# A second half's residual and norm work laid over seven feed-forward tiles instead of four, and a second buffer for its input tokens

## What is computed

```python
def rmsnorm(x, g):
    y = xf * lax.rsqrt(jnp.mean(xf * xf, axis=-1, keepdims=True) + RMS_EPS)
    return (y * g.astype(jnp.float32)).astype(x.dtype)
...
def swiglu(h, w_gu, w_down):
    g, u = jnp.split(h @ w_gu, 2, axis=-1)
    return (jax.nn.silu(g) * u) @ w_down
...
        x = x + gt_m * rmsnorm(y, g_mix_post[l])
        h = rmsnorm(x, g_ffn_pre[l]) * (1.0 + sc_f) + sh_f
        x = x + gt_f * rmsnorm(swiglu(h, ffn_w_gu[l], ffn_w_down[l]), g_ffn_post[l])
```

## Time and profile before

| | us |
|---|---|
| median of 3 runs | 1573.87 |
| lowest and highest of them | 1563.5, 1577.33 |
| the profiled execution | 1572.86 |
| its span | 1571.1 |
| PE busy in the span | 1437.6 |
| DVE busy in the span | 766.0 |
| POOL busy in the span | 637.7 |
| mean granted TensorE clock | 0.957 |

### The profile page before, as it was taken

One profiled execution on the slowest core, in us unless ns is written; L12 is line 12 of the kernel. 1 busy time (PEld: TensorE's weight loads), 2 busy tenths in 40 slices (PEclk: granted clock), 3 DMA queues, 4 the chain that ended last, 5 costly groups with the idle time before them and its releaser, 6 DMA issues.

```text
span 1571.1 us, 20512 instructions
## 1 busy us (share of the span) xinstructions
PE 1437.6 (92%) x7695; PEld 1168.9 (74%) x7695; DVE 766.0 (49%) x1045; ACT 534.0 (34%) x837; POOL 637.7 (41%) x301
## 2 busy tenths in 40 slices
PE   4777999989998999989888999999999999999994
PEld 1356776879987777767666888878877888887883
DVE  5567435894673878635878121123247211121235
ACT  4534274222212666643331232222222222232221
POOL 2524122162153644074533444445554444444450
PEclk9898999999999899989989999999999999999996
DMA  7653200312312344343312333323333433333331
GB/s 278 197 187 126 56 28 27 123 52 64 99 40 63 109 121 125 96 147 94 121 57 78 94 94 105 93 80 96 98 100 93 135 94 94 94 94 93 96 91 54
DMA packets 236698, 156.55 MB, mean 100 GB/s; under 512 B 11043, under 2 KB 222385, under 8 KB 236507
## 3 DMA queue, kind: packets, MB, share of 16 engines
q1 hardware_dynamic: 233189, 143.46, 30.4%
q10 hardware_dynamic: 3446, 12.24, 2.3%
HBM read 147.25 MB, written 8.81 MB: 99 GB/s over the span
## 4 chain that ended last, share of the span: by engine, by line
PE 75%; DVE 15%; ACT 4%; POOL 3%; issue 2%; DMA 1%; ACTq 1%; DVEq 0%; POOLq 0%
PE ps L1731 30%; PE ps L1736 15%; PE ps L1857 10%; PE ps L1860 5%; PE ps L2013 2%; PE ps L1979 2%; PE ps L1990 1%; POOL w_lo L1024 1%; PE ps L1779 1%; PE ps L1873 1%; DVE x L1630 1%; DVE a_f L1595 1%; DVE pr L1577 1%; DVE nrm L1597 1%; DVE a_f L1629 1%
## 5 line engine op out<-in xcount | busy, mean ns | idle before, releaser
L1008 POOL TENSOR_TENSOR w_lo<-raw,w_hi 128x1024 fp32r<-128x1024 f32 x152 | 371.8, 2447 | 447.3 <-ACT w_hi L639 447.2
L1731 PE MATMUL ps<-hb_hi,w_hi 128*128 128x512 f32 x832 | 331.6, 399 | 24.4 <-DVE g_t L1654 10.8
L1731 PE MATMUL ps<-hb_lo,w_hi 128*128 128x512 f32 x832 | 329.2, 396 | 0.0
L639 ACT ACTIVATE w_hi<-raw 128x1024 fp32r<-128x1024 f32 x152 | 160.0, 1053 | 186.6 <-PE ps L1736 180.1
L1736 PE MATMUL ps<-hb_hi,w_lo 128*128 128x512 f32 x832 | 210.2, 395 | 1.9 <-POOL w_lo L1008 1.9
L1731 PEld LDWEIGHTS ps<-hb_hi,w_hi 128*128 128x128 f32 x832 | 159.6, 192 | 63.5 <-DVE g_t L1654 12.4
L1024 POOL TENSOR_TENSOR w_lo<-raw,w_hi 128x1024 fp32r<-128x1024 f32 x22 | 95.1, 4324 | 228.1 <-ACT w_hi L779 228.1
L1736 PEld LDWEIGHTS ps<-hb_hi,w_lo 128*128 128x128 f32 x832 | 157.9, 190 | 37.1 <-POOL w_lo L1008 2.3
L1731 PEld LDWEIGHTS ps<-hb_lo,w_hi 128*128 128x128 f32 x832 | 159.7, 192 | 33.0
L1857 PE MATMUL ps<-ha_hi,w_hi 128*128 128x512 f32 (+2 forms) x432 | 164.6, 381 | 3.4 <-ACT w_hi L779 3.4
L1857 PE MATMUL ps<-ha_lo,w_hi 128*128 128x512 f32 (+2 forms) x432 | 161.8, 375 | 0.0
(11 more groups left out here) (245 smaller groups left out, 2115.8 us busy)
## 6 DMA issues: line engine op xcount, KB each, us to landing
raw<-in_ffn_w_gu SPq DMA_DIRECT2D x88, 512.0 KB, 3.8
ada1x<-in_ada_w SPq DMA_DIRECT2D x32, 512.0 KB, 4.0
raw<-in_ffn_w_down SPq DMA_DIRECT2D x32, 512.0 KB, 4.0
raw<-in_w_in SPq DMA_DIRECT2D x22, 512.0 KB, 3.9
ada<-in_ada_w SPq DMA_DIRECT2D x4, 2048.0 KB, 17.9
raw<-in_w_out SPq DMA_DIRECT2D x16, 512.0 KB, 4.1
raw<-in_ffn_w_down SPq DMA_DIRECT2D x16, 384.0 KB, 3.3
raw<-in_ktab SPq DMA_DIRECT2D x8, 512.0 KB, 4.5
```

What stands on the lines that cost most here:

```text
L639: act.activation(w_hi[:, b, :], raw[:, b, :], ACT.Copy).then_inc(hi_done, 1)
L1008: pool.tensor_tensor(w_lo[:, b, :], raw[:, b, :], w_hi[:, b, :].bitcast(F32), ALU.subtract).then_inc(lo_done, 1)
L1731: pe.matmul(dst, w_hi[:, b, k * P:(k + 1) * P], x, start=start and k == 0 and n == 0, stop=False)
```

## The change

In the first half of the feed-forward part (h = 0), seven tiles are written out instead of four, and the loops begin at tile 7. The squares of yo[1] are split in two groups around DVE's part of tile 0, and use sq[:, 1] for the product in place of a_f, since a_f is in use by tile 0. The sum over features 2 moves from tile 1's gate job to tile 2's, and `rstd_of(2)` from after DVE's part of tile 0 to after that of tile 1. The blocks of `add_mixed` are laid down as 1 (before tile 2), 2, 2, 2 and 1 (after tiles 2, 3, 4 and 5), and the transposes follow them. Since transposes now come when a_hi of tiles 4 and 5 is being written, half 1's tokens go to a buffer of their own, which lies where a_hi of tiles 12 to 19 will be. SP's wait before that load (`n_tp, 8`) stays. h = 1 is as before.

```diff
--- before.py
+++ after.py
@@ -247,7 +247,7 @@
 
         x1 = at("x1", S_, [KT, SEQ])
         yo = [at("yo0", P_KV, [KT, HALF]), at("yo1", P_KV + 16384, [KT, HALF])]
-        xr2 = at("xr2", P_HY + 8192, [4, D])
+        xr2 = [at("xr2", P_HY + 8192, [4, D]), at("xr3", P_HY + 24576, [4, D])]
         yd = at("yd", S_ + 32768, [KT, HALF])
         hb3_hi = at("hb3_hi", S_ + 32768, [KT, HALF], F32R)
         hb3_lo = at("hb3_lo", P_KV + 32768, [KT, HALF], F32R)
@@ -587,14 +587,14 @@
             sp.wait_ge(mod_done, 50)
             pair0(J_OUT, src_o)
             for q in range(4):
-                sp.dma_start(xr2[:, q, :], x_tok[q * P:(q + 1) * P, :]).then_inc(xr_ld, 16)
+                sp.dma_start(xr2[0][:, q, :], x_tok[q * P:(q + 1) * P, :]).then_inc(xr_ld, 16)
             phase(J_OUT, 4, src_o)
             pair0(J_OUT + 8, src_o)
             phase(J_OUT + 8, 4, src_o)
             pair0(J_FFN, src_g)
             sp.wait_ge(n_tp, 8)
             for q in range(4):
-                sp.dma_start(xr2[:, q, :], x_tok[(4 + q) * P:(5 + q) * P, :]).then_inc(xr_ld, 16)
+                sp.dma_start(xr2[1][:, q, :], x_tok[(4 + q) * P:(5 + q) * P, :]).then_inc(xr_ld, 16)
             for h in range(2):
                 J0 = J_FFN + h * (GU_JOBS + DOWN_JOBS)
 
@@ -975,9 +975,10 @@
                     act.wait_ge(cols_ok, 1)
                     act.activation(a_hi[:, ds(i, 1), :].rearrange("p a c -> p (a c)"), a_f[:], ACT.Copy).then_inc(g_ah, 1)
 
-                for i in range(4):
-                    gu_tile(i, (lambda: root(2)) if (h, i) == (0, 1) else (lambda: root(4)) if (h, i) == (1, 0) else None)
-                with act.Fori(4, FT) as i:
+                i0 = 4 if h else 7
+                for i in range(i0):
+                    gu_tile(i, (lambda: root(2)) if (h, i) == (0, 2) else (lambda: root(4)) if (h, i) == (1, 0) else None)
+                with act.Fori(i0, FT) as i:
                     gu_tile(i)
                 J0 += GU_JOBS
                 if h == 0:
@@ -1665,19 +1666,26 @@
                 if h == 0:
 
                     dve.wait_ge(n_hl, KT)
-                    for k in range(KT):
-                        dve.wait_ge(acc_free, E_OUT + KT + k + 3)
-                        add_square(yo[1][:, k, :], k, nrm, a_f)
+                    def mixed_squares(ks):
+
+                        for k in ks:
+                            dve.wait_ge(acc_free, E_OUT + KT + k + 3)
+                            link(dve.tensor_tensor(nrm[:] if k == 0 else sq[:, 1, :], yo[1][:, k, :], yo[1][:, k, :], ALU.mult))
+                            if k:
+                                link(dve.tensor_tensor(nrm[:], nrm[:], sq[:, 1, :], ALU.add))
+
+                    mixed_squares(range(0, 4))
+                    gu_tile(0)
+                    mixed_squares(range(4, 8))
                     dve.nop().then_inc(n_sum, 1)
-                    gu_tile(0)
+                    gu_tile(1)
                     rstd_of(2)
-                    gu_tile(1)
-                    add_mixed(1, range(0, 3))
-                    gu_tile(2)
-                    add_mixed(1, range(3, 6))
-                    gu_tile(3)
-                    add_mixed(1, range(6, 8))
+                    add_mixed(1, range(0, 1))
+                    for i, ks in ((2, range(1, 3)), (3, range(3, 5)), (4, range(5, 7)), (5, range(7, 8))):
+                        gu_tile(i)
+                        add_mixed(1, ks)
                     dve.nop().then_inc(n_sum, 1)
+                    gu_tile(6)
                 else:
 
                     rstd_of(4)
@@ -1694,10 +1702,11 @@
                             dve.wait_ge(st_out[q % 2], 16)
                         dve.tensor_copy(xres[:, q % 2, :],
                                         ps[:, 4 + 2 * (q % 2):6 + 2 * (q % 2), :].rearrange("p a b -> p (a b)")).then_inc(o_ev, 1)
-                with dve.Fori(4, FT) as i:
-                    link.loop(i - 4, 1)
+                i0 = 4 if h else 7
+                with dve.Fori(i0, FT) as i:
+                    link.loop(i - i0, 1)
                     gu_tile(i)
-                link.end(FT - 4)
+                link.end(FT - i0)
                 J0 += GU_JOBS
                 if h == 0:
                     rstd_of(3)
@@ -2037,7 +2046,7 @@
                         pe.wait_ge(n_x1, T - 3)
                     k = T % KT
                     for q in range(4):
-                        ins = pe.transpose(ps[:, 2 + T % 4, q * P:(q + 1) * P], xr2[:, q, k * P:(k + 1) * P], ident[:])
+                        ins = pe.transpose(ps[:, 2 + T % 4, q * P:(q + 1) * P], xr2[T // KT][:, q, k * P:(k + 1) * P], ident[:])
                     ins.then_inc(n_tp, 1)
 
             pe.wait_ge(ot_free, 32)
@@ -2081,11 +2090,15 @@
                 if h == 0:
                     gu_tile(0, ready=input_ready)
                     x_turns(range(8, 12))
-                    gu_tile(1, lambda: sum_over_features(2, nrm))
-                    gu_tile(2)
-                    x_turns(range(12, 15))
+                    gu_tile(1)
+                    gu_tile(2, lambda: sum_over_features(2, nrm))
                     gu_tile(3)
+                    x_turns(range(12, 13))
+                    gu_tile(4)
+                    x_turns(range(13, 15))
+                    gu_tile(5)
                     x_turns(range(15, 16))
+                    gu_tile(6)
                 else:
                     gu_tile(0, lambda: sum_over_features(4, nrm), input_ready)
                     gu_tile(1)
@@ -2098,7 +2111,7 @@
                     output_turns(2)
                     pe.wait_ge(o_ev, 2)
                     output_turns(3)
-                with pe.Fori(4, FT) as i:
+                with pe.Fori(4 if h else 7, FT) as i:
                     gu_tile(i)
                 J0 += GU_JOBS
                 if h == 0:
```

## The result

The changed kernel takes 1559.92 us in the median of 16 runs (1552.01 to 1565.97), the kernel before 1568.2 us in the median of 16 (1562.58 to 1577.33). The ratio is 0.9943, with a 95% interval of 0.9924 to 0.9962: by the ratio 8.9 us less (6.0 to 11.9), by the two medians 8.3. The forecast was 1563.9, that is 10.0 less than the 1573.87 of the three runs then known; with 16 runs the median of the kernel before is 5.7 lower.

The account below looks back on a forecast made before the run. Matmuls bound the loop, but DVE sets the pace in the tiles before it. Of 14.8 us lost there, less 2.9 and 1.9 for new losses, 10.0 is gained: 1573.87 - 10.0 = 1563.9, range 1555 to 1573.

Parts of the forecast that it names:

- the sum of 10.0: Total gain forecast by tile 7 in the first feed-forward half: 14.8 - 2.9 - 1.9 us.
- Room: Up to tile 5, PE loses 14.8 us to waits and slow clock; no reordering can bring more.
- Squares: Splitting them lets tile 1 start at 798.7 instead of 802.70; cost ahead of tile 2 is 0, at most some 0.1.
- Norm: New 2.9 us stall before tile 3: a residual block crossed by POOL's w_lo stands between reciprocal and DVE's bank-freeing instruction.
- Residual: From tile 3, two blocks a tile make DVE cycles of 12.13 us; tile 6 starts at 860.2, 1.9 lost.
- Clock: No clock fall taken behind the new 2.9 us stall before tile 3; a fall would cost 1 to 2.5.
- Buffer and rest, at nothing: The separate token buffer, later transposes, moved root and three more written-out tiles add no wait or gain.
- the crossings miss: Rival, chance 0.17: POOL's w_lo miss DVE's SBUF operations before tile 7; gain 12 to 14, time 1561.
- swallowed: Rival, chance 0.08: a transfer or POOL bounds the later loop and eats the gain; time 1573.
- slower: Rival, chance 0.04: stall before tile 3 keeps clock at 1.2 GHz; two tiles at half clock give 1585.
- The rival with the clock: Chance 0.16: clock falls at the stall before tile 3, or DVE cycle exceeds 12.13; gain 5 to 8.5, time 1567.

Follow-up runs that it names:

- again: The changed kernel run once more without any edit, as control; ratio to the kernel before 0.9955.
- split53: Changed kernel with the squares of yo[1] split five and three blocks instead of four and four; 85.1 us from first square to tile 7's gate job, one run.
- act_squares: Changed kernel with residual blocks 2, 2, 2, 2 after tiles 2 to 5, yo[1] squares split five and three, residual squares on ACT; ratio to before 0.9903.
- before_filler: Kernel before with four unused matmuls of ones added on PE behind tile 0's transposes, where it idles; ratio to the kernel before 0.9999.
- blocks_332: Changed kernel with the residual's blocks back at three, three and two after tiles 2, 3 and 4; ratio to the kernel before 0.9985.
- buffer_alone: Kernel before with only half 1's input tokens moved to the second buffer; ratio to the kernel before 1.0006.
- changed_5: The changed kernel without any edit, run again with more rounds; ratio to the kernel before 0.9942.
- block0_later: Changed kernel with residual block 0 moved behind DVE's part of tile 2, blocks 2, 2, 2, 2 after tiles 2 to 5; ratio to the kernel before 0.9961.
- filler: Changed kernel with four unused matmuls of ones added on PE ahead of tile 3, where it idles; ratio to the kernel before 0.9960.

## Why the prediction held, step by step

The time, 1559.92, lies in the range of 1555 to 1573, and the likeliest of the forecasts came true (faster, within 1%). It is 4.0 under the 1563.9, since the three runs from which the forecast started had a median 5.7 too high; the sum of 10.0 itself stands against 8.6 in M and 8.9 in the runs. What brings the gain and what the new stall is were foretold; the clock was not, and both of the things by which the prediction said that it would be wrong were seen: slow matmuls in tile 3, in 3.6 of its 12.6 us, and squares that reach past 809, with tile 2 waiting. That the sum is within 1.4 all the same is in part luck: what it missed at the room (0.5), ahead of tile 2 (1.0) and by the clock (1.7) was made up in part by a residual that cost 1.6 less and a stall that cost 0.6 less than reckoned. The steps, with the times as they would be in the frame of the kernel before (4.9 added to those of the profile after):

- *Room.* 14.8 was 0.5 too much: the sum with ones costs PE 0.9 and not 0.45. Tile 2 took 11.9 with it (805.75 to 817.68). The kernel has one matmul there, which leaves two records; their step had been read as the cost of one matmul.
- *Squares.* Tile 1 at 798.7: right (793.8, that is 798.7). "Cost 0, with at most some 0.1" ahead of tile 2: wrong, it is 0.9. The prediction had written down that two crossings would carry the squares to 809 and then took it that this fits. By its own figures, 805.2 and twice 2.08, it is 809.4, that is 0.5 past the 808.9 at which L1654 was needed. They ended at 809.8. That term is mis-sized by 0.8.
- *Norm.* The mechanism was exact: L1611 is crossed by the w_lo that began 0.5 us earlier, and from the sum with ones to tile 3 it takes 10.5, as reckoned (813.3 to 823.8; 809.51 to 820.02 in the profile after). The wait is 2.2 for 2.9, since the sum held PE 0.5 longer than reckoned and the row counts idle time only from the end of the last matmul, 0.2 behind the step at which the next could start. Tile 3 starts at 824.9 for 823.8, since tile 2 was itself late. The price without the crossing, 0.8, was reckoned wrongly: with L1610 at its 0.75 the three operations end at 821.4, PE starts at 822.1 and the stall is 1.2.
- *Residual.* Cycles of DVE of 10.3, 14.5 and 11.8 (829.55, 844.08 and 855.92 after 819.28), in which the 14.5 holds a wait of 2.67 for PE. 12.13 was near for the last. Of the 1.9 to be lost only 0.2 showed: in the first cycle a single operation was crossed (10.3 is under PE's 11.3), and PE, not DVE, set the pace, the more so as tile 3 was slow.
- *Clock.* "I take no fall" was the step that failed. It fell in all three profiles, for 1.7. It rested on two rows with no fall, 2.40 us idle and 2.04 at 847.26, and the first of them was one outcome of two, as the last section shows. The fall was priced (1 to 2.5) but given to a rival of 0.16.
- *Buffer and rest, at nothing.* Right for the buffer (94.3 for 94.5 with it alone); of the rest nothing was seen.
- *The rivals.* Of "the crossings miss", "swallowed" and "slower" nothing was seen. The rival with the clock (0.16), gain 5 to 8.5, came to pass in its mechanism, and the 8.6 lies at its upper end; the DVE cycle longer than 12.13 did not. Tile 7 began at 872.6, for 871.

The lost parts in M add up: 14.3 of room, less 1.0 ahead of tile 2 (wait and a slow first matmul), 2.3 ahead of tile 3, 1.7 in it, 0.3 ahead of tile 6 and 0.3 in starts and rounding is 8.7, for 8.6 measured.

## What to carry to other kernels

When one engine's side work delays the instruction that frees another's buffer, give each step of the pipeline only what fits in the slack that it has (here two blocks of a residual nearly fit: L1655 to L1655 took 11.8 in the last cycle, crossings included, where PE takes 11.3 to 11.8 a tile with its transposes). Put nothing between the end of a long chain, as sum, root and reciprocal, and the instruction that frees the buffer. An idle time of two or three microseconds on TensorE, as those of 2.2 to 4.1 here, is to be priced twice, as the wait and as slow matmuls behind it; two rows with no fall are not evidence that there will be none. A step of a sum that "just fits" with a known collision counted in should be carried on to the microsecond, or kept as a cost.

## What the runs showed of the hardware that was not expected

**The same idle time, with and without a fall of the clock.** In the second half, ahead of tile 2, PE waits 2.40 or 2.41 for DVE in every one of the 13 profiles. In before, the changed kernel, again and split53 full clock followed; in the nine others it fell. The wait in PE's timeline of again:

```profile
1185.11 0.50 PE L1740 MATMUL ps<-hb_hi,w_hi 128*128 128x512 f32 x1 [2.41 <-DVE g_t L1655]
```

The 11 us behind it, clock 1.00:

```profile
1185.00:1196.00 11.00, 10.89 (x48) 8.94 (x48) 9.88 (x9) 3.13 (x4) 5.26 (x2) 1.00 0.16 48
```

The same wait in act_squares:

```profile
1172.56 0.80 PE L1751 MATMUL ps<-hb_hi,w_hi 128*128 128x512 f32 x1 [2.40 <-DVE g_t L1666]
```

The 11 us behind it, clock 0.84:

```profile
1172.00:1183.00 11.00, 10.44 (x39) 8.52 (x40) 9.81 (x11) 3.12 (x4) 4.37 (x2) 0.84 0.18 52
```

Nor does length alone order the cases elsewhere: 3.19 in before_filler ahead of tile 4 was followed by full clock, 3.19 in blocks_332 ahead of tile 5 by a slow tile, 2.19 in the changed kernel by a slow tile each time. And the pair of waits of 0.66 and 1.45 ahead of tile 3 of the kernel before was followed by a fall there and in buffer_alone, but not in before_filler, nor in blocks_332 one tile later. What else decides (what PE did before, or where in time the wait falls) is open; no run here separates the two. Behind the 2.41 of the second half, the three profiles of the changed kernel had full clock in two and a fall in the third (changed_5), whose cost the next wait of PE took in. The Trainium skill ("TensorE: Matmul & The Clock Gate", Part 1) says of the release of the throttle that its point varies from run to run; that the fall behind one and the same wait comes or stays out is what these profiles add.

**The clock behind the change differs too.** The first job of the down projection starts after a wait of 2.02 in the changed kernel and 2.05 in block0_later, at the same distance from tile 7 (166.2 and 166.4). PE's timeline of the changed kernel:

```profile
1033.95 0.49 PE L1740 MATMUL ps<-a_hi,w_hi 128*128 128x512 f32 x1 [2.02 <-ACT w_hi L639]
```

The stretch around it:

```profile
1032.00:1037.00 5.00, 3.05 (x13) 2.55 (x14) 2.85 (x3) 3.47 (x4) 2.39 (x1) 1.00 0.10 31
```

PE's timeline of block0_later:

```profile
1029.69 0.49 PE L1739 MATMUL ps<-a_hi,w_hi 128*128 128x512 f32 x1 [2.05 <-ACT w_hi L639]
```

The stretch around it:

```profile
1028.00:1033.00 5.00, 3.31 (x10) 2.66 (x11) 3.14 (x3) 3.18 (x4) 2.39 (x1) 0.80 0.07 21
```

With clock 1.00 around this wait the next sum with ones comes 290.6 after tile 7, with 0.80 it comes at 292.4. A second such place is the down projection of the second half. Together they spread the stretch behind tile 7 from 688.2 to 693.4 in 13 profiles, though no instruction of it differs. The changed kernel had 688.4, 688.4 and 688.2, act_squares 693.4 and 691.4. That would account for what block0_later and act_squares, with 2.6 and 5.5 us less in M than the changed kernel, lack of it in their ratios; it was seen in their profiles alone, not in the runs that make the ratios. That it is the clock is read from the rows. Whether a saving ahead moves the outcome is not shown: the kernel before fell at the first place (next sum with ones 292.2 after tile 7) and buffer_alone, with the same waits ahead, did not (290.6), so two programs with the same M differ as well.

**A matmul of plain float32 costs PE twice its recorded step.** Each leaves two records of 0.59, begun 0.45 apart. Four of ones with a 128x512 tile ("x8" in the row of filler) took 3.6 us in filler and before_filler, 0.9 each, where one of the reduced type takes 0.23.
